# A hybrid decoder step on one core: the last quarter rounded ahead of the tables, softplus ahead of a convolution, dt turned inside a unit, the first decay rows on GpSimd's queue

## The reference, cut to what matters

```python
n1 = rmsnorm(x, norm_mix)
proj = n1 @ w_in
z, xbc, dt_raw, sc_b, sc_c, sc_h, gate_a, gate_b = split_last(proj, IN_SPLITS)
xbc_c, xbc_state = causal_dwconv(xbc, xbc0, ssm_conv_w, ssm_conv_b)
xs, Bm, Cm = split_last(jax.nn.silu(xbc_c), ...)
dt = jax.nn.softplus(dt_raw + ssm_dt_bias)
A = -jnp.exp(ssm_a_log)
# ssd_scan, per chunk of 128 tokens:
Acum = jnp.cumsum(dt * A, axis=2)
Lmat = jnp.exp(jnp.where(causal, Acum[:, :, :, None] - Acum[:, :, None], -jnp.inf))
Wm = CB[..., None] * Lmat * dt[:, :, None]
decay_end = jnp.exp(Acum[:, :, -1:] - Acum)
# ... the mixers are merged, then the MLP, the embedding, and
y_prompt = rmsnorm(yp, norm_final)
```

## Time and profile before

| what | value |
|---|---|
| median of the three runs | 2907.64 us |
| the profiled execution | 2908.34 us, of which the span of instructions is 2906.6 us |
| granted clock of TensorE, mean | 0.997 |
| TensorE (matmuls) busy | 2871.0 us, 99% of the span |
| VectorE, ScalarE, GpSimd busy | 1717.3, 1182.6, 281.7 us |
| DMA | 457.33 MB, mean 157 GB/s |
| chain that ended last | TensorE 96%, VectorE 2%, ScalarE 1% |

### The profile page before, as it was taken

One profiled execution on the slowest core, in us unless ns is written; L12 is line 12 of the kernel. 1 busy time (PEld: TensorE's weight loads), 2 busy tenths in 40 slices (PEclk: granted clock), 3 DMA queues, 4 the chain that ended last, 5 costly groups with the idle time before them and its releaser, 6 DMA issues.

```text
span 2906.6 us, 53235 instructions
## 1 busy us (share of the span) xinstructions
PE 2871.0 (99%) x20052; PEld 2803.9 (96%) x20052; DVE 1717.3 (59%) x2165; ACT 1182.6 (41%) x1745; POOL 281.7 (10%) x447
## 2 busy tenths in 40 slices
PE   7999999999999999999999999999999999999998
PEld 6899999999999999999999999999999999999998
DVE  7676766767667655455455555655555555555564
ACT  4554544535445433333333334533333333333443
POOL 2211212112121200000000001000000000000100
PEclk9999999999999999999999999999999999999999
DMA  7566565665656565555555555555545555545463
GB/s 202 159 182 179 153 195 148 181 172 158 191 152 182 162 177 151 147 153 148 145 145 151 153 149 150 145 146 152 151 145 154 149 144 150 153 144 152 137 177 109
DMA packets 753280, 457.33 MB, mean 157 GB/s; under 512 B 14633, under 2 KB 747233, under 8 KB 752625
## 3 DMA queue, kind: packets, MB, share of 16 engines
q1 hardware_dynamic: 679433, 414.21, 50.5%
q10 hardware_dynamic: 73096, 39.39, 4.9%
q0 software_dynamic: 672, 2.66, 0.2%
HBM read 430.73 MB, written 25.47 MB: 157 GB/s over the span
## 4 chain that ended last, share of the span: by engine, by line
PE 96%; DVE 2%; ACT 1%; DMA 0%; issue 0%; POOL 0%; ACTq 0%; SPq 0%; DVEq 0%; POOLq 0%
PE ps L1567 29%; PE ps L1569 29%; PE ps L1568 29%; PE ps L1783 1%; PE ps L1774 1%; PE ps L1935 1%; PE ps L1953 1%; PE ps L1949 0%; PE ps L1804 0%; PE ps L1912 0%; PE ps L1679 0%; PE ps L1689 0%; DVE wlo L1003 0%; PE ps L1680 0%; DVE nt L1035 0%
## 5 line engine op out<-in xcount | busy, mean ns | idle before, releaser
L1567 PE MATMUL ps<-n_hi,whi 128*128 128x320 f32 x4144 | 1288.0, 311 | 1.9 <-issue 1.1
L1568 PE MATMUL ps<-n_lo,whi 128*128 128x320 f32 x4144 | 1282.0, 309 | 0.0
L1569 PE MATMUL ps<-n_hi,wlo 128*128 128x320 f32 x4144 | 1281.9, 309 | 0.0
L1003 DVE TENSOR_TENSOR wlo<-raw,whi 128x1024 fp32r<-128x1024 f32 x746 | 923.9, 1249 | 493.9 <-ACT whi L670 493.0
L670 ACT ACTIVATE whi<-raw 128x1024 fp32r<-128x1024 f32 x746 | 783.8, 1057 | 878.4 <-PE ps L1569 824.9
L1567 PEld LDWEIGHTS ps<-n_hi,whi 128*128 128x128 f32 x4144 | 779.2, 188 | 5.2 <-issue 2.6
L1568 PEld LDWEIGHTS ps<-n_lo,whi 128*128 128x128 f32 x4144 | 779.2, 188 | 0.6
L1569 PEld LDWEIGHTS ps<-n_hi,wlo 128*128 128x128 f32 x4144 | 779.0, 188 | 0.0
L1567 PE MATMUL ps<-c_hi,whi 128*128 128x320 f32 x1728 | 534.9, 310 | 0.5 <-DVE c_lo L1120 0.5
L1569 PE MATMUL ps<-c_hi,wlo 128*128 128x320 f32 x1728 | 534.1, 309 | 0.0
L1568 PE MATMUL ps<-c_lo,whi 128*128 128x320 f32 x1728 | 534.1, 309 | 0.0
(11 more groups left out here) (292 smaller groups left out, 1790.4 us busy)
## 6 DMA issues: line engine op xcount, KB each, us to landing
raw<-in_w_in SPq DMA_DIRECT2D x322, 512.0 KB, 5.1
raw<-in_w_ffn_gate SPq DMA_DIRECT2D x88, 512.0 KB, 4.2
raw<-in_w_ffn_up SPq DMA_DIRECT2D x88, 512.0 KB, 5.0
raw<-in_w_ffn_down SPq DMA_DIRECT2D x88, 512.0 KB, 4.2
raw<-in_w_ssm_out SPq DMA_DIRECT2D x64, 512.0 KB, 4.3
h<-in_state_ssm ACTq DMA_DIRECT2D x32, 512.0 KB, 5.8
out_ssm_sample<-hn ACTq DMA_DIRECT2D x32, 512.0 KB, 4.4
raw<-in_w_sc_out SPq DMA_DIRECT2D x32, 512.0 KB, 4.3
```

The source lines that it names most:

```text
L1003: tt(wlo[slot][:], raw[slot][:], whi[slot][:].bitcast(F32), SUB).then_inc(lo_split, 1)
L1567: mm(out, w_h, x_h, start=first, stop=False)
L1568: mm(out, w_h, x_l, start=False, stop=False)
L1569: return mm(out, w_l, x_h, start=False, stop=last)
```

## The change

Five edits. (1) In the prologue ScalarE rounds the last quarter (`n_hi`) ahead of the six table copies instead of behind them. (2) The first part of softplus, with its Exp, moves from the step behind unit x0 into that unit: on VectorE ahead of the convolution of x0, on ScalarE ahead of the copies into `xpad` and the two state loads. (3) In group 0 the six turns of dt move on TensorE from between x2 and x3 to the middle of x3, between its two pieces; the step `dturn`, which now holds only VectorE's four copies, moves behind x3. (4) The first decay rows are read back by GpSimd's queue, at the start of its step `decay`, instead of SyncE's queue behind the load of piece 14, with semaphores of their own; the seven later groups stay on SyncE. (5) The last two tiles are squared each by itself as it is ready, and the sums on TensorE are regrouped: three parts, then one.

```diff
@@ ssm_steps
-        head = (x(1) + [("dtend", 0)] + x(2) + [("dturn", 0)] + x(3) + [("dtab", 0)] + x(4)
+        head = (x(1) + [("dtend", 0)] + x(2) + x(3) + [("dturn", 0), ("dtab", 0)] + x(4)
                 + [("bc", 0), ("decay", 0)] + x(5) + [("clamp", 0)])
...
+        def loaded(eng, seg, g, first, later):
+
+            if seg.start == 0:
+                eng.wait_ge(first, 32)
+            else:
+                eng.wait_ge(later, 32 * g)
...
@@ SyncE
-                    if seg.name == "ssm" and seg.start == 0 and pos == 10:
-                        sp.wait_ge(rows_saved, 16 * 3)
-                        load_decays(it)
                     if seg.name == "ssm" and seg.start and pos == 6:
-                        load_decays(it)
+                        load_decays(sp, it, acum_loaded, ea_loaded)
...
@@ ScalarE
                     if h < 3:
                         first_split(h + 1)
-                    if h == 2:
+                    if h == 3:
                         for n, (dst, bank, col, width) in enumerate(TAB_COPIES):
...
+            def last_tile(it, j):
+
+                act.wait_ge(ple_added, 4 * it + j + 1)
+                act.wait_ge(sq_added, ADDED[4] + 7)
+                activate(sq_pair[1][:, j - 2, :], final[:, j, :], ACT.Square).then_inc(sq_ready, 1)
...
-                elif kind == "dtstart":
-                    act.wait_ge(dt_min, 1)
-                    activate(wm[0:HEADS, 2, 0:NT], wm[0:HEADS, 1, 0:NT], ACT.Exp).then_inc(dt_exp, 1)
-                    act.wait_ge(cols_loaded, 16 * 3)
-                    activate(hvec[:, 2:3], hvec[:, 1:2], ACT.Exp).then_inc(a_exp, 1)
...
                 elif kind == "unit" and step[1] == "x":
+                    if seg.name == "prologue":
+                        act.wait_ge(dt_min, 1)
+                        activate(wm[0:HEADS, 2, 0:NT], wm[0:HEADS, 1, 0:NT], ACT.Exp).then_inc(dt_exp, 1)
+                        act.wait_ge(cols_loaded, 16 * 3)
+                        activate(hvec[:, 2:3], hvec[:, 1:2], ACT.Exp).then_inc(a_exp, 1)
                     act.wait_ge(multiplied, unit_end(seg, it, pos))
...
@@ VectorE
                 elif kind == "dtstart":
+                    pass
+                elif kind == "unit" and step[1] == "x" and seg.name == "prologue":
                     w = dt_parts()
...
                     own(ts(w[1], w[4], 1.0 / 15, None, MUL))
+                    convolve(g, j)
...
@@ GpSimd
                 elif kind == "decay":
 
+                    if seg.start == 0:
+                        pool.wait_ge(rows_saved, 16 * 3)
+                        load_decays(pool, it, first_acum_loaded, first_ea_loaded)
                     wait(pool, f_ready, 4 * g)
                     pool.wait_ge(hcol_ready, g + 1)
-                    pool.wait_ge(acum_loaded, 32 * (g + 1))
+                    loaded(pool, seg, g, first_acum_loaded, acum_loaded)
...
@@ TensorE
             def unit(seg, it, step, pos):
                 bank = bank_free(seg, it, step)
                 for half in range(2):
+                    if half and seg.name == "ssm" and seg.start == 0 and step[1:] == ("x", 3):
+                        turn_dt()
                     slot = piece_ready(seg, it, pos + half)
...
-                    last_sums(sq_sum, True)
+                    pe.wait_ge(sq_ready, SQUARES[4] + 8)
+                    last_sums([sq_sum[:, 0, :], sq_sum[:, 1, :], sq_pair[1][:, 0, :]], True, False)
                     turn_rows(KM // 4, range(3, 4))
-                    pe.wait_ge(sq_ready, SQUARES[4] + 8)
-                    last_sums(sq_pair[1], False).then_inc(sq_summed, 1)
+                    pe.wait_ge(sq_ready, SQUARES[4] + 9)
+                    last_sums([sq_pair[1][:, 1, :]], False, True).then_inc(sq_summed, 1)
```

More of the change, by code:

```diff
@@ L974, in tasks @@
                     activate(sig_a[:, j % 2, :], ps[:, j, 0:NT], ACT.Sigmoid).then_inc(sigs, 1)
-                    if j % 2:
+                    if seg.start == KM // 4 - 1 and j >= 2:
+                        last_tile(it, j)
+                    elif j % 2:
                         last_squares(it, j // 2)
@@ L1156, in keep, with convolve @@
                               ps[0:NS, bank, 2 * HEADS:3 * HEADS].rearrange("p (g h) -> p g h", g=GROUPS))
+            def convolve(g, j):
+                dve.wait_ge(xpad_filled, 6 * g + j + 1)
+                dve.wait_ge(xpast, 6 * g + j + 1)
+                dve.wait_ge(gcol_ready, g + 1)
+                wait(dve, xs_ready, 6 * g + j - 1)
+                taps(cv[:, j % 2, 0:N_CX], xpad[j % 2], [gcol[:, k, j:j + 1] for k in range(K_X)],
+                     gcol[:, K_X, j:j + 1], N_CX).then_inc(conv_done, 1)
             def dt_parts():
@@ L1208, in tasks @@
                 elif kind == "unit" and step[1] == "x":
[L1209 to L1213, removed]
-                    taps(cv[:, j % 2, 0:N_CX], xpad[j % 2], [gcol[:, k, j:j + 1] for k in range(K_X)],
-                         gcol[:, K_X, j:j + 1], N_CX).then_inc(conv_done, 1)
+                    convolve(g, j)
                 elif kind == "ssd1":
@@ L1644, in bank_free, with turn_dt @@
                     return j
+            def turn_dt():
+                pe.wait_ge(dt_done, 1)
+                for bank, i in ((2, 0), (3, 1)):
+                    for c in range(3):
+                        rows = P if c < 2 else NS
+                        last = turn(ps[0:rows, bank, c * HEADS:(c + 1) * HEADS], wm[0:HEADS, i, token_rows(c)],
+                                    ident[0:HEADS, 0:HEADS])
+                last.then_inc(dt_turned, 1)
             def unit(seg, it, step, pos):
@@ L1726, in turn_rows, with last_sums @@
                         last.then_inc(y_turned, 1)
-            def last_sums(part, first):
+            def last_sums(parts, first, end):
                 for c in range(3):
                     rows = P if c < 2 else NS
-                    for t in range(2):
-                        last = mm(ps[0:rows, c, 0:1], part[:, t, token_rows(c)], ones[:, 0:1],
-                                  start=first and t == 0, stop=not first and t == 1)
+                    for n, part in enumerate(parts):
+                        last = mm(ps[0:rows, c, 0:1], part[:, token_rows(c)], ones[:, 0:1],
+                                  start=first and n == 0, stop=end)
                 return last
@@ L1865, in tasks @@
                     last.then_inc(multiplied, 1)
-                elif kind == "dturn":
-                    pe.wait_ge(dt_done, 1)
-                    for bank, i in ((2, 0), (3, 1)):
-                        for c in range(3):
-                            rows = P if c < 2 else NS
-                            last = turn(ps[0:rows, bank, c * HEADS:(c + 1) * HEADS], wm[0:HEADS, i, token_rows(c)],
-                                        ident[0:HEADS, 0:HEADS])
-                    last.then_inc(dt_turned, 1)
                 elif kind == "dtab":
```

33 lines of the change are left out of this document (17 added, 16 removed).

## The result

The changed kernel takes 2913.08 us (median of 19 runs, 2910.92 to 2913.64). The kernel before takes 2908.04 us (19 runs beside them, 2906.39 to 2909.71). That is less than the 5.8 us (0.2%) which the prediction took as telling a kernel from no change, so its class "slower than 2913.5" (0.65) did not come, but the class within (0.30). The profiled execution of after took 2912.87 us with a span of 2911.2, against 2906.6 before: +4.6.

The account below looks back on a forecast made before the run. TensorE, busy 99% of the span, was taken as the bound, so only its waits and clock count. Terms -2.05 + 4.2 + 3.1 + 3.5 + 0 = +8.75 us gave a forecast of 2916.5 us, range 2908.0 to 2922.0.

Parts of the forecast that it names:

- slower than 2913.5: Whole kernel: outcome class of a time above 2913.5 us, given a chance of 0.65.
- the class within: Whole kernel: outcome class between slower than 2913.5 and faster by over 5.8 us, given a chance of 0.30.
- The new wait at `dtab`: TensorE ahead of `dtab`: waits 5.9 us for VectorE's copies, held behind x3's splits and convolution; `dtab` begins at 75.0.
- The clock behind it: `dtab` and x4: the clock falls to half behind the new 5.9 us wait, costing +4.2 us, bounds 0 and 5.7.
- The place of the decay rows: Ahead of `ssd1`: loads issued later, behind `hcol` on GpSimd, raise TensorE's wait from 1.3 to 4.5 us, +3.1.
- Rival (b): Decay-row loads: GpSimd's queue is slow, 4.1 us more, 2920.6 us; chance 0.12.
- The clock behind that wait: Turns of `ssd1` and unit z1: the clock falls behind the 4.5 us wait, costing +3.5 us, else 0.
- rival (a): Waits at `dtab` and `ssd1`: clock holds at one (2912.9 us, chance 0.2) or both (2908.7 us, chance 0.1).
- the rule on the clock: TensorE's waits: 1.97 us of idling keeps the clock, 4.41 us costs it, so longer waits count as falls.
- (c): At `dtab`: copies not held, wait below 2 us, clock high; 2903.0 us, at best 2901.0; chance 0.06.
- (d): Whole kernel: waits removed and added cancel, so the change does nothing; the lower end of rival (a).

Follow-up runs that it names:

- experiment 6: Kernel before with only the last quarter rounded ahead of the table copies: 2904.6 us, ratio 0.9991.
- experiment 7: Kernel before with only the last quarter rounded first and dt turned inside x3, VectorE's copies staying ahead of x3's splits: 2901.51 us, ratio 0.9978.
- 3: Changed kernel with VectorE's copies put back ahead of x3's splits and the first decay rows loaded by SyncE: 2901.35 us, ratio 0.9978.
- experiment 4: Changed kernel with the decay-row loads still on GpSimd's queue but issued earlier, in its step `dtab`: 2909.72 us, ratio 1.0005.
- experiment 10: Changed kernel with 36 idle matmuls ahead of the wait for the copies at `dtab`: 2909.86 us, ratio 1.0008.
- experiment 5: Changed kernel with 24 idle matmuls ahead of the wait for the copies at `dtab`: 2911.5 us, ratio 1.0010.
- 2: Changed kernel with the first decay rows issued by SyncE again, early in x4: 2909.82 us, ratio 1.0004.
- experiment 1: Changed kernel with VectorE's four copies put back ahead of x3's splits, decay rows left on GpSimd's queue: 2904.29 us, ratio 0.9988.
- 9: Kernel of 8 with 6 idle matmuls ahead of the dt turns in x3 and 3 behind: 2900.99 us, ratio 0.9977.
- 8: Kernel of 3 with GpSimd's first multiplication of states waiting for the convolution of x5: 2901.67 us, ratio 0.9978.
- 11: Changed kernel with 36 idle matmuls ahead of the wait at `dtab` and 18 ahead of that at `ssd1`: 2922.39 us, ratio 1.0051.
- 12: Changed kernel with 34 idle matmuls ahead of the wait at `dtab` and 14 ahead of that at `ssd1`: 2917.0 us, ratio 1.0031.

## Why the prediction was right, and what was off

**Edit 1, -2.1: right.** The last quarter is rounded at 37.90 and x1 has no new wait. From the first matmul of the first quarters to the second half of x2 TensorE takes 29.5 us in after (26.48 to 55.99) and 31.7 before (26.67 to 58.34). Alone the edit measured -2.9, for the reasons given in experiment 6.

**Edit 2, 0, and edit 5, 0: right** (experiment 7 against 3). The last sums of after stand without a gap, as before.

**Edit 3, the turns inside x3: right in its waits, its gain too high.** A wait of 0.9 and one of 0.56 (forecast 0.9 and 0.3), 1.5 us for 4.4. With the copies left in place edit 3 brings 3.1 us (7 against 6), where the prediction counted 5.9. It took the slow clock as gone for good, 2.6 us; in 6 less of it was left to gain, and in 7 the clock fell in x3 itself. The sum did not suffer, since `dtab` was held by the copies.

**The new wait at `dtab`: right in place and cause, mis-sized.** I said 5.9 us, it was 4.19. The copies ended at 74.7, against the 75.0 forecast. TensorE came late, at 70.67 instead of 69.1: the second half of x3 took 5.32 us instead of 3.8, with the clock at half rate behind two short waits. The wait shrank by what TensorE lost, so `dtab` came at 74.86, the 75.0 of the sum. Where TensorE arrived with the clock up, the wait was 5.64 (experiment 4).

**The clock behind it, +4.2: too high for after, right for its neighbours.** +3.1 was measured. I priced all of `dtab` at half rate, at +2.9; but the fall came 1.1 us behind its start, so `dtab` lost 1.5, and x4 the other 1.6. Filling the wait won the same 3.05 back (experiment 10). In the other kernels with that wait `dtab` and x4 lost 3.1 (5), 3.7 (2) and 4.7 (4) against the 10.15 us of before. The forecast lies inside that spread, and the bounds of 0 and 5.7 held.

**The place of the decay rows, +3.1: mis-sized.** +1.7 was measured. The chain was as described: issue behind `hcol`, 6.7 us to `gnrm`, 4.9 of GpSimd's work, the slow convolution, 4.9 to TensorE. I had 7.2 for the landing, 0.5 too much; 5.7 for GpSimd's part, where it took 5.2; and half a us for going between two ends, where the convolution followed at once. The 1 MB load took 5.8 us by itself, as against 5.7 from SyncE's queue before. The estimate of 4.4 us from the Trainium skill, "DMA: Bandwidth & Descriptors", section on the anatomy of one DMA from GpSimd, is 1.4 us below that, so the measurement decides against it here. Rival (b), 4.1 us more for the landing, was not met either.

**The clock behind that wait, +3.5: mis-sized.** +1.6 was measured: 1.06 in the turns (2.59 for 1.53), the rest in the unit behind. The wait was 2.87 instead of 4.5. I had counted the clock as fallen because 4.5 is just beyond the 4.41 that had cost it; a wait of 2.87 was for the prediction the case of rival (a), "fall short". It fell all the same, and in 10, with 3.16, it did not. So that it fell in after was in part luck.

**The weakest step is therefore the rule on the clock**: that 1.97 us keep it and 4.41 lose it, so that the length of a wait decides. Fall and no fall overlap. It held behind 3.16 (experiment 10), and fell behind 2.87 (after), 3.02 and 3.29 (5 and 1, at `ssd1`) and 2.08 (5, at `dtab`), and once with nothing longer than 0.31 near (9). Behind the same pair of waits in x3, 0.92 and 0.56, it fell in five of eleven profiled executions (after, 2, 3, 7 and 10) and held in six (1, 4, 5, 8, 11 and 12). What it costs when it falls varies as well: 3.4 us at half rate or 6.8 in after, 3.4 or 6.49 behind the same 4.4 us (6 and before). From these runs a likely share of each wait can be told, not a threshold.

**Rivals.** (c), faster, was the right map of what to mend: its condition, copies not held by x3's convolution, is experiment 1, and 3 reaches the 2901 us that it gave at best. (d) is refuted by the interval above 1. (a) with one fall gave 2912.9, nearer to the 2913.08 than the forecast, but by luck: both falls came, each of them smaller. In the sum the two clock terms and the place of the rows were too high by 4.4 us together, and the tail too low by 0.5. The 0.5 is no effect of the change that could be told: the same stretch took from 2793.8 (experiment 7) to 2794.9 (8) in the kernels without a long filling.

**Best version.** Edits 1 and 3 with the copies in their old place and the loads on SyncE: 2901.4 us, 6.5 us or 0.22% below before, with or without edits 2 and 5. The additions of 8 and 9 bring nothing more that can be told.

## What to carry to other kernels

When a step is moved inside another so that its wait is shared, look at everything that is bound to it on the other engines: here TensorE's turns were worth 3.1 us inside x3, and VectorE's four copies, moved with them behind a convolution that can't start before x3 ends, cost 8.5. A wait at the head of dense work can be paid twice, once as idle time and again as clock: here 4.2 us of waiting had 3.1 of clock behind them, which idle matmuls won back without shortening the wait. It need not be so; 3.16 us in another place cost no clock. Loads moved to another engine's queue stand where that engine's program has come to, not where their data is ready.

## What the runs showed of the hardware

- The granted clock fell to half behind an idle time of 2.08 us (experiment 5, at `dtab`) and held behind one of 3.16 us (10, at `ssd1`), in kernels that differ by twelve idle matmuls.
- Idle matmuls in place of 4.2 us of waiting took 3.2 us off the whole kernel in the median, although the work behind them began 0.5 us later.
- VectorE's convolution steps over 344 columns take 0.58 to 0.60 us alone and 1.24 to 1.25 beside GpSimd's multiplication of states, shown by moving GpSimd alone (8 against 3).
- The kernels with 48 and 54 matmuls more at 70 to 103 us show 18 more loads of instructions and two stalls of some 3 us more than 1100 us later; the one with 36 more shows one load more than before and no such stall. That the number of matmuls is the cause is not shown.
